# Moving the second tile of a 31-tap convolution from VectorE to GpSimd, and two copies on ScalarE two projections ahead

## What is computed

```
u = x @ w_in[l]
z, xbc, dt_raw, q, k, v, qi, ki, wi, glu = split(u)
xbc = silu(causal_dwconv(xbc, prev, ssd_conv_w, ssd_conv_b))       # 4 taps, 6 tiles
...                                                                # state-space scan, top-k attention
gl = glu[..., :256] * sigmoid(glu[..., 256:])
c  = causal_dwconv(gl, prev, cc_conv_w, cc_conv_b)                 # 31 taps, 256 channels = 2 tiles
y_cc = silu(layer_norm(c, cc_ln_g, cc_ln_b))
mix = concat([y_ssd, y_att, y_cc]) @ w_out[l]                      # then a feed-forward block
```

## Time and profile before

| | |
|---|---|
| time, median of 3 runs | 3491.53 us (3487.83 to 3495.37) |
| the profiled execution, its own time | 3503.6 us |
| its span | 3501.8 us |
| mean granted share of the PE clock | 0.954 |
| busy over the span | PE 93%, PEld 75%, DVE 54%, ACT 35%, POOL 19% |

### The profile page before, as it was taken

One profiled execution on the slowest core, in us unless ns is written; L12 is line 12 of the kernel. 1 busy time (PEld: TensorE's weight loads), 2 busy tenths in 40 slices (PEclk: granted clock), 3 DMA queues, 4 the chain that ended last, 5 costly groups with the idle time before them and its releaser, 6 DMA issues.

```text
span 3501.8 us, 49906 instructions
## 1 busy us (share of the span) xinstructions
PE 3247.3 (93%) x19418; PEld 2641.0 (75%) x19418; DVE 1900.5 (54%) x3006; ACT 1212.0 (35%) x2294; POOL 663.5 (19%) x663
## 2 busy tenths in 40 slices
PE   7899999887999999999989998997888999999997
PEld 4444466555899999999854444774578999999996
DVE  5579784325654534435455996843357544435345
ACT  4256714243332212212133656243325212212123
POOL 0000000021043333424200000000201433334340
PEclk9899999787999999999999999997889999999998
DMA  4101105325011111111121110241430111111111
GB/s 137 46 30 36 35 19 159 92 76 170 1 40 48 37 53 42 43 53 36 62 47 43 36 35 26 89 135 44 143 104 14 37 54 41 44 50 36 55 37 67
DMA packets 168248, 205.77 MB, mean 59 GB/s; under 512 B 61185, under 2 KB 136258, under 8 KB 166850
## 3 DMA queue, kind: packets, MB, share of 16 engines
q1 hardware_dynamic: 163394, 201.43, 19.2%
q10 hardware_dynamic: 4608, 1.05, 0.1%
HBM read 189.33 MB, written 13.08 MB: 58 GB/s over the span
## 4 chain that ended last, share of the span: by engine, by line
PE 68%; DVE 12%; issue 8%; ACT 5%; SPq 3%; DMA 2%; ACTq 0%; POOL 0%; DVEq 0%; POOLq 0%; PEldq 0%
PE PS L794 45%; PE PS L775 5%; DVE MIX L1773 4%; SPq L451 3%; PE PS L807 2%; PE PS L876 2%; ACT X L1405 2%; DVE WORK L1962 1%; PE PS L834 1%; PE PS L1004 1%; DMA RING<-cache_k 1%; PE PS L969 1%; PE PS L1070 1%; ACT WORK_parts L1403 1%; PE PS L1152 1%
## 5 line engine op out<-in xcount | busy, mean ns | idle before, releaser
L794 PE MATMUL PS<-WORK_parts,WHIGH_parts 128*128 128x352 f32 x3936 | 813.7, 328 | 19.6 <-DVE MIX_parts L2277 11.2
L794 PEld LDWEIGHTS PS<-WORK_parts,WHIGH_parts 128*128 128x128 f32 x3936 | 675.2, 190 | 23.6 <-issue 23.6
L794 PE MATMUL PS<-WORK_parts,RING_parts 128*128 128x352 f32 x3024 | 659.1, 326 | 0.0
L775 PE MATMUL PS<-X,RING 128*128 128x512 f32 (+1 forms) x1824 | 601.5, 492 | 22.4 <-ACT MIX L1474 9.5
L775 PEld LDWEIGHTS PS<-X,RING 128*128 128x128 f32 x1824 | 303.7, 193 | 320.5 <-issue 318.4
L794 PEld LDWEIGHTS PS<-WORK_parts,RING_parts 128*128 128x128 f32 x3024 | 522.5, 189 | 0.0
L1773 DVE SCALAR_TENSOR_TENSOR WORK<-WORK,VEC 128x1072 f32<-128x1072 f32 (+1 forms) x236 | 483.7, 2050 | 8.4
L1354 ACT ACTIVATE WORK<-PS 128x32 f32<-128x32 f32 (+8 forms) x444 | 193.0, 490 | 811.4 <-PE PS L794 564.9
L515 POOL TENSOR_TENSOR RING_parts<-RING,WHIGH_parts 128x1024 fp32r<-128x1024 f32 (+2 forms) x184 | 373.0, 2027 | 448.1 <-ACT WHIGH_parts L1354 447.6
L794 PE MATMUL PS<-X_parts,WHIGH_parts 128*128 128x352 f32 x2016 | 436.1, 324 | 0.0
L1771 DVE TENSOR_SCALAR WORK<-WORK,VEC 128x1072 f32<-128x1072 f32 (+1 forms) x90 | 70.6, 784 | 515.4 <-ACT WORK L1354 515.4
(11 more groups left out here) (335 smaller groups left out, 3917.7 us busy)
## 6 DMA issues: line engine op xcount, KB each, us to landing
RING<-w_up SPq DMA_DIRECT2D x88, 512.0 KB, 3.6
RING<-cache_k SPq DMA_DIRECT2D x256, 128.0 KB, 2.1
RING<-cache_v SPq DMA_DIRECT2D x256, 128.0 KB, 2.1
RING<-w_in SPq DMA_DIRECT2D x46, 512.0 KB, 3.6
RING<-w_down SPq DMA_DIRECT2D x80, 256.0 KB, 2.7
RING<-cache_kidx SPq DMA_DIRECT2D x192, 32.0 KB, 1.8
WORK<-w_out SPq DMA_DIRECT2D x12, 512.0 KB, 6.7
MIX<-xT SPq DMA_DIRECT2D x3, 1408.0 KB, 9.8
```

Of the source, the lines that this page charges most:

```text
L775: mm = pe.matmul(job_psum(n, w, first=first), stationary(k), moving(k)[:, first:first + w], start=k == 0, stop=k == k_tiles - 1)
L794: mm = pe.matmul(thirds(n)[:, third, :], a, x[:, third * THIRD:(third + 1) * THIRD], start=k == 0 and part == 0, stop=k == tiles - 1 and p ...
```

## The change

POOL takes the 31 taps of the convolution's tile 1 and DVE keeps those of tile 0. On POOL each tap but the first is two instructions, a product into a scratch tile (the two halves of `WHIGH`, free in this stage) and a sum onto the accumulator. The taps stand in seven groups in POOL's list: four ahead of the state copies of XBC+0, four behind the copies of each of XBC+0 to XBC+4, and the last seven behind those of XBC+5. Each instruction waits for the one before. On ACT the two biased copies move from ahead of the mean job to ahead of the job Z+3.

```diff
+CC_READY_AT = ("in", T_Z + 3)
+TAPS_TO = [0, 4, 8, 12, 16, 20, 24, CC_W]
...
-        cc_convolved = sem("cc_convolved")
+        cc_convolved = [sem("cc_convolved_by_vector"), sem("cc_convolved_by_gpsimd")]
...
+                tap = Steps(pool, pool_tap)
+                w = CC_LEN - CC_H
+                convolved, tapped = ACC[1][:, 0:w], WHIGH_PLAIN.rearrange("p a b -> p (a b)")[:, 0:w]
+
+                def convolve_taps(n):
+
+                    for k in range(TAPS_TO[n], TAPS_TO[n + 1]):
+                        weight = v(V_CCW + CC_W + k)
+                        if k == 0:
+                            tap.then_wait(pool.tensor_scalar(convolved, CC[:, 1, 0:w], weight, 1.0, ALU.mult, ALU.mult))
+                            continue
+                        tap.then_wait(pool.tensor_scalar(tapped, CC[:, 1, k:k + w], weight, 1.0, ALU.mult, ALU.mult))
+                        ins = pool.tensor_tensor(convolved, convolved, tapped, ALU.add)
+                        if k < CC_W - 1:
+                            tap.then_wait(ins)
+                        else:
+                            ins.then_inc(cc_convolved[1], 1)
+
+                await_freed(pool, JOB[("in", T_GLU + 1)])
+                convolve_taps(0)
                 for t in range(6):
                     await_freed(pool, JOB[("in", T_XBC + t)])
                     pool.tensor_copy(SSDO[:, t, 0:SSD_H], XBC[:, t, SEQ:SEQ + SSD_H])
                     pool.tensor_copy(by_sample(SSDO[:, t, SSD_H:], SSD_H),
                                      samples(XBC[:, t, SSD_S0:], SSD_SEG, DEC_SEQ, SSD_H)).then_inc(saved, 1)
+                    convolve_taps(t + 1)
...
                 def project(n):
                     name = JOBS[n]
-                    if name == ("mean", "cc"):
+                    if name == CC_READY_AT:
                         for t in range(2):
-                            act.wait_ge(cc_convolved, t + 1)
+                            act.wait_ge(cc_convolved[t], 1)
                             act.activation(MIX[:, 6 + t, 0:SEQ], ACC[t][:, 0:SEQ], ACT.Identity, bias=v(V_CCB + t))
...
                 def convolve_conformer():
-                    for t in range(2):
-                        await_freed(dve, JOB[("in", T_GLU + t)])
-                        yield from convolve_by_taps(ACC[t][:, 0:CC_LEN - CC_H], CC[:, t, :], CC_W, V_CCW + t * CC_W,
-                                                    cc_convolved)
+                    await_freed(dve, JOB[("in", T_GLU)])
+                    yield from convolve_by_taps(ACC[0][:, 0:CC_LEN - CC_H], CC[:, 0, :], CC_W, V_CCW, cc_convolved[0])
```

More of the change, by code:

```diff
@@ L390, in build @@
         vector_step, scalar_step, pool_step = sem("vector_step"), sem("scalar_step"), sem("pool_step")
+        pool_tap = sem("pool_tap")
         hist_set, saved, conv_done, silu_done, cc_ready = (sem(n) for n in (
             "history_set", "states_saved", "conv_done", "silu_done", "cc_ready"))
-        cc_convolved = sem("cc_convolved")
+        cc_convolved = [sem("cc_convolved_by_vector"), sem("cc_convolved_by_gpsimd")]
         ranked, scan_tried, scan_counted, scan_found, scan_next = (sem(n) for n in (
@@ L1457, in project @@
                                            ACT.Identity, bias=v(V_CCB + t)).then_inc(cc_ready, 1)
+                    if name == ("mean", "cc"):
                         norm_squares("cc")
```

## The result

The changed kernel takes 3630.32 us (median of 4 runs, 3622.32 to 3632.08), the kernel before 3493.45 (4 runs, 3487.83 to 3498.57) beside it: 1.0388 times as long, 95% interval 1.0365 to 1.0411. The prediction said 3576 us and 3508 to 3625: the direction was right, the delay too small, and the time lies 5 us outside the range. The profiled executions span 3629.2 us and 3501.8 us, 127.4 apart.

A forecast was written before the change was run, and what follows sets the result against it. DVE's list was taken to bound PE in the stage; 27.5 + 8 + 6, say 42 us later in each of two layers, adds 84 to 3503.6, giving 3587.6 profiled, less 12.1: 3576 us, range 3508 to 3625.

The forecast's parts named there:

- DVE's list bounds the stage: From XBC+3 on PE moves at DVE's pace; each us that Z+0's second-bit request (379.8 us) moves, PE moves too.
- Exclusion: DVE and POOL share a port lock, so one waits for the other's whole instruction; together 167.5 us where there were 140.
- POOL's durations: On 1296 columns a POOL product takes 1.34 us and a sum 3.0 us, 132 us for all 31 taps.
- The ledger's total of waiting: Locked DVE and POOL work up to 379.8 us, plus 8 us uncovered and 6 us small steps: 42 us later a layer.
- The 35.4 us of taps that go, counted whole: Taps leaving DVE's list ahead of 379.8 us: 22 at 34.5 us plus 0.9 us for the first.
- Nothing behind Z+0: The lateness at Z+0 is neither given back nor increased up to Q+0; all of it shifts as a whole.
- the copies at nothing: ACT's biased copies, moved ahead of Z+3, cost 2.9 us within ACT's slack; the mean's saved wait is worth nothing.
- Lower PE clock: Rival: PE waiting some 8 us in each of eight jobs runs slower behind stops, perhaps 2 us a layer; no chance given.
- POOL as the bound: Rival, 15%: POOL's list itself sets the pace and copies come late; 3612 us at a likelier 60 a layer, up to 3667.
- No lock: Rival, 10%: POOL's taps lie beside DVE's, PE runs without the four stops, 10.3 us a layer gained, 3471 us.
- half a lock: Rival, 8%: only POOL's sums lock, or small steps slip through; stage within some 5 us a layer, 3480 to 3510 us.
- sums at 2.3 us: Rival, 17%: POOL's sums take 2.3 us, 16 us less a layer, 26 later instead, 3543 us.

The follow-up runs named there:

- e5: Kernel before, with DVE taking no extra taps behind the XBC jobs' bits, so 12 taps move to the Z and K jobs: 3483.14 us, ratio 0.9954.
- e3: Kernel before, DVE keeping both tiles' taps, plus the changed kernel's POOL products and sums writing only to scratch: 3667.58 us, ratio 1.0494.
- e4: Changed kernel with POOL's products and sums replaced by fills that read nothing, tile 1's convolution left out: 3505.24 us, ratio 1.0030.
- e2: Changed kernel without POOL's 61 tap instructions, one zero fill instead, so nobody convolves tile 1: 3477.36 us, ratio 0.9954.
- e12: Changed kernel in which DVE takes only two taps of tile 0 and leaves out the other 29: 3596.91 us, ratio 1.0280.
- e1: Kernel before with only ACT's biased copies moved ahead of Z+3, DVE keeping both tiles' taps: 3510.69 us, ratio 1.0047.
- e11: Changed kernel with POOL's 31 taps in one go, ACT doing the small XBC history copies: 3643.39 us, ratio 1.0408.
- e8: Changed kernel with POOL's 31 products but without its 30 sums: 3512.26 us, ratio 1.0047.

## Why the prediction was right or wrong

- **DVE's list bounds the stage: right.** e5 moves 12 taps out of it and PE's stops go.
- **Exclusion: right**, and shown from three sides: 84.6 us a layer with nothing taken from DVE (e3), 13.8 by nearly the same POOL time without reads (e4 against e2), 2.33 us for a five-column step in the rows above.
- **POOL's durations: products right (1.34 us), sums too high.** Alone they take 2.48 us, not 3.0; the row of L515, whose output is of another type (fp32r), was the wrong neighbour. The Trainium skill's figure (GPSIMD Engine Reference, "Performance versus the Vector engine") had given an estimate of 2.85 us, high as well. By itself this makes the forecast too large, by some 23 x 0.52 = 12 us a layer, and so hides a part of what the other terms lack.
- **The ledger's total of waiting: nearly right, by two errors that cancel.** The forecast was 42 + 35.4 = 77.4 us that POOL adds to DVE's list. Measured: each group's growth in mean times its count (43.5 - 24.2, 33.1 - 28.2 and 18.6 - 4.7 for the convolutions; 15 each of L2031, L2000, L2038 and L2035 from some 0.17 to 0.957, 0.910, 0.804 and 0.761; 3.3 for two smaller forms) is 82.5 us. The sums were cheaper, but all 31 taps fell into the stretch, not 24, since it became longer: POOL's last one ended at 434.2 us.
- **The 35.4 us of taps that go, counted whole: this step failed.** The mechanism of the forecast was right, and this is the term of its sum that was mis-sized most: "27.5 us more" takes all of the 35.4 us off the stretch, and the ledger hid all of ACT behind DVE and POOL ("ACT is no more than 62% busy"). But DVE and ACT take turns: DVE's request, then some 4.7 us of counts on ACT, in the XBC jobs also a read-out and a silu behind them, then DVE's next step. The taps had filled that time (DVE waited 0.3 us there before, and 0.3 us in e3). Without them DVE's idle time in the stretch (239.8 to 440.4 us, below) is 200.6 - 180.2 = 20.4 us instead of 6.2, 14.2 us more. e3 and e12 show the same: of the 43.7 us that tile 1's taps take beside POOL only 23.0 come off DVE's list and 19.3 off Q+0, and leaving 18 taps of tile 0 out doubles the wait for ACT. The windows of the changed kernel, as in the earlier trace rows:

```profile
239.80:440.40 200.60, 137.01 (x381) 67.77 (x380) 180.23 (x238) 85.75 (x176) 138.08 (x73) 0.81 0.08 23
```

- **Nothing behind Z+0: failed by a little; the copies at nothing: right here.** From Z+0's second bit to Q+0 it is 74.4 us instead of 70.7. PE has more left to do at that bit: it starts Z+2 6.8 us ahead of it instead of 13.1, and then runs four jobs in a row in 65.11 us. Up to the end of K+1 that makes 4.1 us more, and the way from there to Q+0 is 0.4 shorter. ACT waits for PE there, so the copies are covered, though e1 alone loses 2.5 us by them.
- **Lower PE clock: a little more than priced (2 us a layer).** The granted clock is 0.81 in the stretch instead of 0.99; behind the last stop the four jobs run at 0.96 and take 65.1 us (63.6 in the second layer), where e2's PE, which never stops, needs 62.1 for four (16 jobs in 248.5 us), and Q+0's own job is 1.5 and 2.5 us longer.
- **The sum again:** 42 + (82.5 - 77.4) + 14.2 + 3.7 = 65.0 us a layer, against 65.3 measured (63.8 in the second layer).
- **From the profile to the median.** I took 12.1 us off, because the profiled execution of before lay that much above its runs. The changed kernel's lies 0.6 above its median (3631.0 and 3630.3), and before's runs beside e11 reach 3508. The 12 us were scatter, not an offset; without them the forecast is 3588, and the range would just have held.
- **POOL as the bound (15%), with 3612 us at a likelier 60 a layer, came nearest in number but not in cause:** Z+3's copies wait for nothing, POOL ends at 434.2 us and they start at 467.54, and POOL in one go (e11) makes it no faster. *No lock* (10%) and *half a lock* (8%) fall by e3 and e8; *sums at 2.3 us* was right on the sums (2.48, and 2.34 of hold) and wrong on the time.

## What to carry to other kernels

Work that is taken from an engine is worth only what the next engine in its loop leaves: where two engines take turns (a request, a count, a request), subtract from the gain the time in which the removed work had covered the other's turn. When work goes to GpSimd beside VectorE, count each GpSimd instruction that reads SBUF as time on VectorE's list whenever that list has two-input or copy-like instructions waiting, small ones too. And before moving work to another engine, ask whether it must stand where it stands: one number that puts twelve taps behind later jobs gained 0.46%, where moving 31 taps to an idle engine lost 3.9%. Compare a moment of two traces from a start that both share: here the stage began up to 4.4 us apart by chance, more than several of the differences that were asked for.

## What the runs showed of the hardware

- A VectorE step on 5 to 32 columns (0.17 us alone) waits out a GpSimd instruction as a tap does, up to 2.3 us: four such steps of a bit cost DVE 41 us of the 82.5 in a stretch.
- GpSimd's fills (1.21 us for 1296 columns) pass beside VectorE's two-input instructions without a loss (1569 ns), and hold up its tensor_scalar of five columns (1.20 us under a fill instead of 0.17).
- GpSimd's dependent instructions follow each other at 0.1 us (297.36 to 297.45 in the rows above), and a VectorE instruction that waits gets its turn in between: POOL's next one then takes longer (1.69 and 3.38 to 3.61 us instead of 1.34 and 2.48).
- How the same GpSimd instructions are grouped in time (six stops of PE or three) changed the end by 3.7 us in 65.
